# Five beats of a hand-written order are moved: selection and gates of one token tile, four early chunk loads, one small normalization

## What is computed

```python
# peer layer, per token, 8 heads, 16 experts each out of 16384 (128 x 128 keys)
q = (xt @ w_pq).reshape(T, 8, 2, 128)
s = einsum('thpd,hpnd->thpn', q, subkeys)
top_s, top_i = top_k(s, 16)                     # twice 16 of 128
best_s, best_pos = top_k(cand_s, 16)            # 16 of the 256 sums -> expert, gate
act = gelu(einsum('thkd,td->thk', peer_u[expert], xb)) * softmax(best_s)
out = einsum('thk,thkd->td', act, peer_v[expert])

# block 2's spatial gating unit (sgu), v is 256 x 512
vn = (v - mean(v)) * rsqrt(var(v) + eps) * ln_g + ln_b
y_b = u * (W_s vn + b)                          # over blocks of 128 tokens
```

## Time and profile before

| | |
|---|---|
| median of 3 runs | 2184.94 us (2179.93 to 2187.13) |
| the profiled execution | 2187.13 us, of which 2185.3 us are its span |
| busy: PE, PEld, DVE, ACT, POOL | 90%, 83%, 69%, 48%, 40% of the span |
| mean granted TensorE clock | 0.970 |
| DMA | 595.75 MB, mean 273 GB/s |
| block 1's dense chunks on TensorE | 476.7 to 863.4 us of the span |
| block 1's gates of t = 1, then of t = 0, on TensorE | 656.2 to 749.7, 784.6 to 860.0 us |

### The profile page before, as it was taken

One profiled execution on the slowest core, in us unless ns is written; L12 is line 12 of the kernel. 1 busy time (PEld: TensorE's weight loads), 2 busy tenths in 40 slices (PEclk: granted clock), 3 DMA queues, 4 the chain that ended last, 5 costly groups with the idle time before them and its releaser, 6 DMA issues.

```text
span 2185.3 us, 34980 instructions
## 1 busy us (share of the span) xinstructions
PE 1975.9 (90%) x13778; PEld 1823.9 (83%) x13778; DVE 1500.7 (69%) x2790; ACT 1047.4 (48%) x2012; POOL 863.9 (40%) x626
## 2 busy tenths in 40 slices
PE   6999998969878899999998999877998899899997
PEld 6999988969878899888787889876897789788886
DVE  5643431388899856898877333276697987699887
ACT  5455442123336556555555552122333668566656
POOL 0000000167677733676630000066777624355640
PEclk9999999989999999999999999999999899999999
DMA  5433454899999987899973434699999866799985
GB/s 216 137 131 122 157 193 171 320 365 379 367 409 354 331 264 250 295 325 320 327 263 132 171 119 156 241 385 411 381 401 399 318 198 211 258 318 317 310 290 192
DMA packets 150785, 595.75 MB, mean 273 GB/s; under 512 B 19271, under 2 KB 20935, under 8 KB 134750
## 3 DMA queue, kind: packets, MB, share of 16 engines
q1 hardware_dynamic: 97374, 408.94, 52.5%
q0 software_dynamic: 53248, 184.58, 22.8%
HBM read 592.40 MB, written 1.05 MB: 272 GB/s over the span
## 4 chain that ended last, share of the span: by engine, by line
PE 58%; DMA 18%; DVE 10%; issue 6%; ACT 4%; POOL 3%; DVEq 0%; POOLq 0%; ACTq 0%
PE bank L993 13%; PE bank L1032 9%; DMA ut_sb<-in_ut_dram 6%; PE bank_n L1032 6%; PE bank L957 4%; PE bank L1012 4%; DMA big_sb<-in_u_dram,idx_sb 4%; DMA nt_sb<-in_vl_dram,idx_sb 4%; PE bank L611 4%; DMA junk_sb<-in_vl_dram,idx_sb 4%; PE bank L612 3%; PE bank L613 3%; PE bank L854 2%; DVE v_lo L1645 2%; PE bank L706 1%
## 5 line engine op out<-in xcount | busy, mean ns | idle before, releaser
L993 PE MATMUL bank<-nt_sb,ut_sb 128*128 128x128 f32 x4096 | 510.8, 282 | 59.4 <-DMA ut_sb<-in_ut_dram 58.6
L993 PEld LDWEIGHTS bank<-nt_sb,ut_sb 128*128 128x128 f32 x4096 | 488.4, 197 | 71.5 <-DMA ut_sb<-in_ut_dram 56.2
L2300 POOL DMA_INDIRECT big_sb<-in_u_dram,idx_sb x256 | 270.7, 1058 | 248.5 <-ACT big_sb L1144 127.0
L2300 POOL DMA_INDIRECT nt_sb<-in_vl_dram,idx_sb x172 | 245.9, 1430 | 249.0 <-DVE x_sb L1651 130.7
L2264 POOL TENSOR_TENSOR sm_sb<-sm_sb,vec_sb 128x1 f32<-128x1 f32 (+2 forms) x24 | 19.5, 814 | 714.6 <-DVE sm_sb L1648 714.6
L1144 ACT ACTIVATE big_sb<-bank 128x512 f32<-128x512 f32 (+13 forms) x284 | 131.9, 477 | 354.3 <-PE bank L993 126.3
L2070 DVE CUSTOM_DVE_ANT_0 big_sb<-big_sb,bank_n 128x1024 f32<-128x1024 f32 x170 | 205.3, 1209 | 85.1 <-DMA big_sb<-in_u_dram,idx_sb 84.6
L1144 ACT ACTIVATE v_hi<-nt_sb 128x1024 fp32r<-128x1024 f32 x162 | 172.6, 1065 | 147.8 <-PE bank L1032 59.5
L2321 POOL TENSOR_TENSOR big_sb<-big_sb,nt_sb 128x1024 f32<-128x1024 f32 x86 | 206.5, 2402 | 13.7 <-DMA big_sb<-in_u_dram,idx_sb 12.2
L1144 ACT ACTIVATE big_sb<-big_sb 128x1024 f32<-128x1024 f32 (+2 forms) x132 | 116.5, 885 | 178.2 <-POOL big_sb L2321 164.7
L1645 DVE TENSOR_TENSOR v_lo<-nt_sb,v_hi 128x1024 fp32r<-128x1024 f32 x162 | 197.9, 1221 | 0.0
(11 more groups left out here) (249 smaller groups left out, 4146.3 us busy)
## 6 DMA issues: line engine op xcount, KB each, us to landing
ut_sb<-in_ut_dram SPq DMA_DIRECT2D x256, 512.0 KB, 7.1
big_sb<-in_wall_dram SPq DMA_DIRECT2D x123, 1024.0 KB, 5.2
nt_sb<-in_v_dram SPq DMA_DIRECT2D x154, 512.0 KB, 4.5
sw_sb<-in_v_dram SPq DMA_DIRECT2D x102, 512.0 KB, 4.5
big_sb<-in_u_dram,idx_sb POOLq DMA_INDIRECT x256, 9.6
nt_sb<-in_vl_dram,idx_sb POOLq DMA_INDIRECT x172, 5.4
sw_sb<-in_v_dram SPq DMA_DIRECT2D x8, 320.0 KB, 3.3
nt_sb<-in_v_dram SPq DMA_DIRECT2D x8, 320.0 KB, 3.0
```

What stands on the lines that cost most here:

```text
L993: i = e.matmul(hs(bk, c % 4), UT[:, c % DR, k * 128:(k + 1) * 128], TN[1][:, k, :], start=k == 0, stop=k == 7)
L2300: return e.indirect_dma_start(out, None, table, bass.IndirectOffsetOnAxis(ap=IDX[:, k:k + 1], axis=0))
```

## The change

Five beats or groups of beats move, and with them the place of the instructions in the queues; no instruction's work is changed, except that the bounds between `weigh`, `dense` and ScalarE's copies for t = 1 follow the new beats.

```diff
-T_SEL = {(1, 1): (418, 20), (2, 0): (1239, 34), (2, 1): (1374, 23)}
+T_SEL = {(1, 1): (432, 23), (2, 0): (1239, 34), (2, 1): (1374, 23)}
-T_GATE = {(1, 0): (598, 1.7), (1, 1): (510, 1.7), (2, 0): (1545, 1.7), (2, 1): (1484, 1.7)}
+T_GATE = {(1, 0): (598, 1.7), (1, 1): (540, 1.7), (2, 0): (1545, 1.7), (2, 1): (1484, 1.7)}
...
             def dense(l):                       # SyncE
                 for c in range(128):
-                    yield dense_beat(l, c - DR) + 0.2 if c >= DR else (352, 1250)[l - 1]
+                    yield dense_beat(l, c - DR) + 0.2 if c >= DR else (304.5, 1250)[l - 1]
...
             def sgu(t):                         # TensorE
-                yield (1129, 1196)[t]
+                yield 1123 + 73 * t
...
             def sgu(t):                         # ScalarE
-                yield (1122.5, 1189.5)[t]
+                yield 1116.5 + 73 * t
...
             def sgu(t):                         # VectorE
-                b = (1118, 1185)[t]
+                b = 1112 + 73 * t
...
             def sgu(t):                         # GpSimd
-                yield (1123.5, 1190.5)[t]
+                yield 1117.5 + 73 * t
```

## The result

The changed kernel takes 2198.8 us (median of 4 runs, 2193.2 to 2201.4); the kernel before takes 2182.9 us in the 4 runs beside it (2179.9 to 2187.1). The ratio is 1.0067, 95% interval 1.0040 to 1.0096: 0.7% slower, 14.6 us. The forecast was 2188.0 with a range of 2176 to 2200 and "same" as its likeliest class; the time lies inside the range, near its upper end, and by the forecast's own bounds (0.3%) the class came out as slower. Of its signs of being wrong two came true, one of them by 0.03 us.

What follows compares the result with a forecast made beforehand. Block 1's peer layer was taken as bound by DMA, then VectorE (tile 1's gates), then TensorE. Terms -2.5 - 3 - 3.4 + 8.7 + 3.3 = +3.1 us gave 2188.0 us on the median, range 2176 to 2200.

Steps and rivals of the forecast that it cites:

- signs of being wrong: Block 1: tile 0's gates starting before 775 or after 795, or chunk 0 starting later than 480.
- Early loads: Block 1, dense loads ahead of the first query load: 4.95 us delay, more than covered later; -2.5 us, bounds -5 to +5.
- the relief: Block 1, 430 to 470: 2.10 MB leave the full DMA stretch, giving 5.3 us back to the gathers.
- Selection and waits at the gates' start: Block 1, tile 1: wider selection regains lost DMA time, -3 us; three TensorE waits at the gates' start go, -3.4 us.
- gates later: Block 1, first gate of tile 1 to tile 0's: 40.6 + 92.4 + 4.1, 137.1 us instead of 128.4; +8.7 us.
- The order of limits: Tile 1's 32 gates: VectorE bounds 26 at 3.0 us each, then TensorE sets the pace for six at 2.4 us.
- The first rival: Block 1, tile 1's gates: comparisons no longer held up by GpSimd's products; all gone is 14.3 us, 2173.7; chance 0.16.
- Block 2's `sgu(0)`: VectorE's first part, ahead of load 2's low part, waits for ScalarE's eviction; +3.3 us, bounds 0 to +6.
- the likeliest case: The sum of the terms over blocks 1 and 2: +3.1 us, 2188, own range 2181 to 2194; chance 0.42.
- the second rival: Block 1: the early loads' 4.95 us delay stays and the relief goes unused; 2195.5 us; chance 0.30.
- the clock's bound: Block 2's sgu(0): upper bound +6 us, if the longer pause holds the lower clock for as long again.
- the sign "after 795": Block 1: prediction wrong if tile 0's gates start after 795, meaning the early delay was kept; expected 785 to 790.

Runs made afterwards that it cites:

- the harmless place: Kernel before with block 1's first four dense loads at beat 311, behind the first two query loads, not 352: 2184.1 us, ratio 0.9995.
- nearly all of the products: Kernel before with GpSimd's 43 products of block 1 cut to 64 of 1024 columns, leaving out 15/16 of each: 2163.5 us, ratio 0.9904.
- the single edit: Kernel before with only the four beats of block 2's sgu(0) 6 lower: 2191.6 us, ratio 1.0023.
- a lead of the comparisons: VectorE's comparisons of block 1, tile 1 one step earlier: 2183.2 us in the kernel before, 2188.9 us with selection and gates later.
- Three single versions: Kernel before with: early loads behind two query loads, 0.9995; sgu(0) edit with VectorE's first part at 1115, 0.9989; selection and gates earlier (gates at 502), 0.9994.

## Why the prediction was right or wrong

**Early loads (-2.5 forecast, +3.7 measured, interval -0.4 to +7.7): wrong, and by the medians the larger miss.** The delay itself was right. The first query weights, on the chain of the changed kernel:

```profile
384.01 16.48 DMA big_sb<-in_wall_dram
```

16.48 us to land in place of 10.99 are 5.5 us for a forecast of 4.95. (The Trainium skill, page "DMA: Bandwidth & Descriptors", section "Queues, rings and completion order", says that descriptors are consumed in ring order on each DMA engine; the trace agrees, the wait is that of the bytes put ahead.) The step that failed is "I walked the queue ... and find dense chunk 0 and the dots about 2.5 us earlier than before": no gain from the relief shows. With the loads in the harmless place none showed either. The rival that was named, that the delay stays, is what happened: 3.4 us more than in the profile before were there at tile 0's gates, and the first query, at 398.9, had been 2 to 6 us later than in the six kernels with the loads in their old place. A part that I had not priced is the clock: in the changed kernel the granted clock is 1.00 from 395 to 397 and 0.50 from 400 to 404, in and behind the pause of 6.29 us. There TensorE ran at 1.2 GHz in place of 2.4, and its lag grew from 5.6 us at the first query to 7.3 at the first score product; idle time before the transposes (7.31 us in the earlier trace rows, now 1.03) took about half of it back, as the prediction said: 3.3 us are left at chunk 0.

**Selection and waits at the gates' start (-3 and -3.4), then gates later (+8.7): together +2.3 forecast, +7.2 measured (interval +3.7 to +10.7).** Up to the first gate of tile 1 the step holds. From chunk 0 to that gate the kernel before took 656.17 - 476.7 = 179.5 us, the one with selection and gates later 214.4: 34.9 more, for a forecast of 40.6 - 3 - 3.4 = 34.2. What is off is the sum behind it: 92.4 + 4.1 = 96.5 forecast between the first gates of the two tiles, 100.1 found there, 102.1 in the changed kernel. A part is counted plainly: behind the last two gates at 791.43 stand three chunks and not two, 5.5 us for 4.1. The rest, some 2 us and 4 in the changed kernel, is in the gates, where TensorE's clock is 0.90 to 0.96. The prediction priced each gate by rows from a stretch in which the clock was 1.00 and took over that clock; that this is the whole of the rest isn't shown. The step that failed is thus the size of a term, the 92.4 + 4.1 us for the 32 gates and what stands behind them. The order of limits in it came true: in the changed kernel VectorE is busy without a gap from 720 to 774, and then TensorE, for 17.1 of the last 17.4 us. The -3 for the selection is borne out by the traffic, as said above. In the changed kernel the waits at the gates' start didn't go but changed place: the three of the earlier trace rows are gone, 3.4 us, and in their place TensorE waits 2.21 and 1.45 us at the second and third gate.

**The first rival, hold-ups gone: rightly given little.** In the changed kernel's gates of tile 1 the comparisons stay slow (VectorE's groups, 696.5 to 791.4):

```profile
L1645 DVE TENSOR_TENSOR sw_sb<-cst_sb,ef_sb 128x1024 f32<-128x1024 f32 x16 | 22.9, 1438 | 0.0
...
L1645 DVE TENSOR_TENSOR ab_sb<-cst_sb,ef_sb 128x1024 f32<-128x1024 f32 x7 | 14.0, 2003 | 0.0
L1645 DVE TENSOR_TENSOR row_sb<-cst_sb,ef_sb 128x1024 f32<-128x1024 f32 x8 | 12.5, 1561 | 0.0
```

That is 49.4 us for 31 comparisons, 0.39 of hold-up each against the 0.55 forecast (the 19 us for 30 comparisons that the prediction read are 0.63 each). Its price for all hold-ups, 14.3 us, can't be checked alone: 21 us went with nearly all of the products, but then GpSimd's own time goes too.

**Block 2's `sgu(0)`: right.** TensorE's wait was forecast at 4.8 us and is 4.79 in the single edit, 4.50 in the changed kernel; the low part was forecast to start at 1239.07 and started at 1239.24. The timing gives +5.0 with an interval of +1.3 to +8.5, the length of the stage +3, and the experiment that undoes only VectorE's order takes it all away.

**The forecast as a whole.** Two terms were short, by some 6 us and 5 us, and both on the same side, which made +14.6 of +3.1. The mechanism named for each of the three places was the right one to look at; the likeliest case relied on traffic that would be used because it was free. That the time still lies in the range is in part luck. The range reached up to 2200 for the second rival, which did happen, at 3.7 of the 4.95 us that it named, with the clock's bound on top; the gates' miss of 4.9 us used up the room meant for that bound. And the sign "after 795" came true by the gates at least as much as by the early delay for which it was named.

**What stays open.** Why later gates lengthen the stage ahead of tile 0's gates, and how much of that is TensorE's clock and how much waiting. It is not the hold-ups, and a lead of the comparisons doesn't take it away. A further idea was not tried: up to the gates each chunk waits for its load (2.05 us of work every 2.56), so a gate placed there would fill time that is lost anyway, and one placed later takes time of its own; kernels with fewer bytes in the loads would tell. The waits point that way without showing it. From 480 to 790 TensorE waits for its chunk loads for 16.0 to 21.7 us in the seven kernels with early gates and for 21.0 to 26.0 in the five with later ones, and for VectorE's products for 11.6 to 13.7 and 9.7 to 14.3.

No version beat the kernel before. Three single versions came out at 0.9989 to 0.9995, each with 1 inside its interval.

## What to carry to other kernels

A prefetch belongs behind the loads that the chain waits for: the same four loads two places further down the queue showed no cost, and ahead of them they made TensorE wait 6.1 us in place of 0.8, with +3.7 us in the time (interval -0.4 to +7.7). Free bandwidth is worth something only if an instruction is ready to use it; look for what frees the buffers before a gain is booked. In an in-order queue, look at what a moved instruction waits for, and at what stood behind it: a part of 1.3 us put ahead of another one made TensorE wait 3.3 us longer. And compare stages by their lengths, from one named instruction to another: places counted from the start of the span differed by more than 6 us between profiles of kernels that are equal up to there.

## What the runs showed of the hardware

The clock. TensorE's first queries in the changed kernel, after a wait of 6.29 us, ran for 9.10 us where the same 64 instructions took 7.38 us behind a wait of 0.80 us in the kernel before. In the gates a chunk took 3.04 us at 705.71 in place of 1.95.

A short VectorE product of two SBUF inputs can be held up for far longer than its length. In the kernel with the gates alone, VectorE and then GpSimd:

```profile
744.26 5.54 DVE L1645 TENSOR_TENSOR big_sb<-big_sb,nt_sb 128x240 f32<-128x240 f32 x1
```

```profile
744.86 4.67 POOL L2321 TENSOR_TENSOR big_sb<-big_sb,nt_sb 128x1024 f32<-128x1024 f32 x2
```

GpSimd's two products of 2.34 us ran one behind the other, and VectorE's 128x240 product of two SBUF inputs lasted until both were done; one of 128x208 took 0.36 us in the kernel before. By the records VectorE's product had started 0.60 us ahead of GpSimd's.
